# Activation table sets asked for ahead of their use, and the last scaling in four uneven parts

## The reference

```python
def first_block(x, c, ctx, c_ctx, ...):      # one layer
    h = rmsnorm(x) * (1 + scale) + shift      # modulation from c; the same for ctx with c_ctx
    p = h @ w_in                              # r, k, v, gates, low-rank decay and rate, q, k, v, gates of the second mixer
    # mixer A: RWKV-7 recurrence over 16 heads of 64, forwards and backwards, started from the state of ctx
    decay = exp(-exp(-softplus(-w_log) - 0.5)); kk = k * rsqrt(sum(k*k)); y = scan(...); group norm; silu gate
    # mixer B: chunked gated linear attention, 4 heads, both directions: exp of cumulated log-sigmoids
    mixed = sigmoid(g_a) * (y_a @ w_a) + sigmoid(g_b) * (y_b @ w_b)
    return rmsnorm(x + gate * (mixed @ w_out))
def second_block(x, ...):
    # layer AB: 8 heads of dilated attention, 4 heads of differential attention with an RMS norm per head
    # layer C:  16 heads of blockwise attention (all blocks fit, so causal attention)
    # every layer: softmax (exp), silu gate, output projection, residual
    return rmsnorm(h, final_norm)
```

## Time and profile before

| | |
|---|---|
| three executions | 2341.84, 2342.4, 2343.54 us |
| median | 2342.4 us |
| profiled execution, first to last instruction | 2339.4 us |
| DVE, ACT and POOL busy | 1223.0, 1178.4 and 1344.6 us (52, 50 and 57% of the span) |
| ACT_TABLE_LOADs | 63 of 1283 ns |

### The profile page before, as it was taken

The page is one execution under the profiler, slowest core; times in us unless marked ns, Lnnn a source line. Parts: engine busy times, 40 slices in busy tenths (PEclk is TensorE's granted clock), DMA queues, the critical chain, the costliest instruction groups (busy, mean ns, idle before and its releaser), DMA issues.

```text
span 2339.4 us, 60054 instructions
## 1 busy us (share of the span) xinstructions
PE 2285.5 (98%) x23364; PEld 1944.0 (83%) x23364; DVE 1223.0 (52%) x2449; ACT 1178.4 (50%) x1999; POOL 1344.6 (57%) x566
## 2 busy tenths in 40 slices
PE   6999999999999999999999999999999999999997
PEld 4787788778877888899999888888888888888886
DVE  2478778877783332465565455454434533333332
ACT  3245545554553443554444555555555555555554
POOL 1113123322232434488888877877778877778785
PEclk8999999999999999999999999999999999999999
DMA  9922112211211223366767555555555555555553
GB/s 388 381 90 69 43 61 71 65 46 55 69 65 59 86 93 102 100 242 239 268 244 244 180 171 173 173 171 174 172 171 172 182 166 177 172 177 172 171 181 134
DMA packets 101247, 360.75 MB, mean 154 GB/s; under 512 B 11184, under 2 KB 14768, under 8 KB 101072
## 3 DMA queue, kind: packets, MB, share of 16 engines
q1 hardware_dynamic: 99872, 356.89, 44.6%
q10 hardware_dynamic: 1200, 1.25, 0.2%
HBM read 356.00 MB, written 2.10 MB: 153 GB/s over the span
## 4 chain that ended last, share of the span: by engine, by line
PE 89%; DVE 2%; ACT 2%; issue 1%; DVEq 0%; ACTq 0%
PE ps L223 32%; PE ps L224 16%; PE ps L678 5%; PE ps L196 4%; PE ps L198 4%; PE ps L197 4%; PE ps L680 4%; PE ps L679 4%; PE ps L808 1%; PE ps L793 1%; PE ps L829 1%; PE ps L965 1%; PE ps L843 1%; PE ps L939 1%; PE ps L955 1%; PE ps L984 1%
## 5 line engine op out<-in xcount | busy, mean ns | idle before, releaser
L187 POOL TENSOR_TENSOR wlo<-raw,whi 128x1024 fp32r<-128x1024 f32 x555 | 1339.2, 2426 | 941.3 <-ACT whi L178 898.1
L223 PE MATMUL ps<-acts,whi 128*128 128x512 f32 x3072 | 1088.5, 398 | 1.3 <-DVE acts L2777 1.3
L224 PE MATMUL ps<-acts,wlo 128*128 128x256 f32 x3072 | 856.9, 279 | 0.0
L178 ACT ACTIVATE whi<-raw 128x1024 fp32r<-128x1024 f32 x562 | 591.7, 1054 | 270.2 <-PE ps L224 138.8
L223 PEld LDWEIGHTS ps<-acts,whi 128*128 128x128 f32 x3072 | 576.3, 188 | 132.4 <-DVE acts L2777 1.6
L224 PEld LDWEIGHTS ps<-acts,wlo 128*128 128x128 f32 x3072 | 579.1, 188 | 0.9
L678 PE MATMUL ps<-acts,whi 128*128 128x512 f32 (+1 forms) x560 | 217.1, 388 | 1.8 <-DVE W L1543 0.9
L680 PE MATMUL ps<-acts,wlo 128*128 128x512 f32 (+1 forms) x560 | 189.9, 339 | 0.0
L679 PE MATMUL ps<-acts,whi 128*128 128x512 f32 (+1 forms) x560 | 189.8, 339 | 0.0
L196 PE MATMUL ps<-acts,whi 128*128 128x256 f32 (+1 forms) x576 | 181.7, 315 | 0.0
L198 PE MATMUL ps<-acts,wlo 128*128 128x256 f32 (+1 forms) x576 | 180.0, 313 | 0.0
(11 more groups left out here) (391 smaller groups left out, 3085.0 us busy)
## 6 DMA issues: line engine op xcount, KB each, us to landing
raw<-stream SPq DMA_DIRECT2D x564, 512.0 KB, 3.3
W<-stream SPq DMA_DIRECT2D x64, 512.0 KB, 9.2
graw<-stream SPq DMA_DIRECT2D x32, 512.0 KB, 4.4
W<-xT SPq DMA_DIRECT2D x4, 1024.0 KB, 8.7
XR<-xT SPq DMA_DIRECT2D x16, 128.0 KB, 5.6
outT<-XR SPq DMA_DIRECT2D x4, 512.0 KB, 3.3
cns<-consts SPq DMA_DIRECT2D x1, 928.0 KB, 11.0
cns<-consts SPq DMA_DIRECT2D x1, 896.0 KB, 7.4
```

Source lines behind the costliest of these rows:

```text
L178: nc.scalar.activation(high, raw[slot], ACT.Copy).then_inc(hi_done, 1)
L187: nc.gpsimd.tensor_tensor(wlo[slot], raw[slot], whi[slot].bitcast(F32), ALU.subtract).then_inc(lo_done, 1)
L223: nc.tensor.matmul(both_parts, whi[slot][:, k, :], hl[:, :, k0 + k, :], start=first and k == 0, stop=False)
L224: ins = nc.tensor.matmul(ps[:, bank, 0:T], wlo[slot][:, k, :], hl[:, 0, k0 + k, :], start=False, stop=last and k == UK - 1)
```

## The change

Two names of table sets are defined: `LN_EXP` (logarithm and exp) and `EXP_TANH`. ACT is told to load a set with `preload_act_table_set`, an instruction of its own in ACT's queue with no wait. The end's scaling is cut into parts of 2, 2, 4 and 4 tiles on DVE, and SyncE stores each of them by itself; POOL's four tiles are stored after the third part.

```diff
+        LN_EXP, EXP_TANH = "natural_log_exp_and_others", "exp_and_others"
@@ act_inverse (8 times)
             turned(4, 1)
+            nc.scalar.preload_act_table_set(EXP_TANH)
             token_key(1)
@@ act_scan (7 times: not for the last pair)
             solved(2)
+            nc.scalar.preload_act_table_set(LN_EXP)
             act_pad_r(act, j)
@@ act_gla
                 if i == 0:
                     act_square(act, PAIRS - 1)
+                if i == 0:
+                    nc.scalar.preload_act_table_set(LN_EXP)
                 G["gk_mm"].wait(act, 2 * i + 2)
...
                     nc.scalar.activation(zg[:, T * n:T * n + T], z_held(i, n), ACT.Tanh, scale=0.5).then_inc(G["tz"].sem, 1)
+                nc.scalar.preload_act_table_set(LN_EXP)
                 if i + 1 < GH:
                     hi(15)
@@ out_phase, act_
+                            if i == KT // 2 - 1 and n == 0 and base == S_OUT3:
+                                nc.scalar.preload_act_table_set(LN_EXP)
                             tile(i, n)
                         if i == KT // 2 - 1 and k == 5:
-                            nc.scalar.activation(small[:, 106:107], kst_[:, 3:4], ACT.Ln if base == S_OUT3 else ACT.Sqrt)
+                            if base != S_OUT3:
+                                nc.scalar.activation(small[:, 106:107], kst_[:, 3:4], ACT.Sqrt)
@@ dve_final
+        END_PARTS = ((4, 2), (6, 2), (8, 4), (12, 4))
-            for k in range(4, KT, 4):
-                nc.vector.tensor_tensor(XR[:, k:k + 4, :], XR[:, k:k + 4, :],
-                                        ps[:, 7, 0:T].unsqueeze(1).broadcast_to([P, 4, T]), ALU.mult).then_inc(N["x"].sem, 1)
+            for k, n in END_PARTS:
+                nc.vector.tensor_tensor(XR[:, k:k + n, :], XR[:, k:k + n, :],
+                                        ps[:, 7, 0:T].unsqueeze(1).broadcast_to([P, n, T]), ALU.mult).then_inc(N["x"].sem, 1)
@@ sp_store
-            for k in (4, 8, 0, 12):
-                if k:
-                    S["out3"]["x"].wait(sp, k // 4)
-                else:
-                    S["out3"]["tab"].wait(sp, 1)
-                sp.dma_start(outT[:, k:k + 4, :], XR[:, k:k + 4, :]).then_inc(stored, 16)
-            sp.wait_ge(stored, 64)
+            for m, (k, n) in enumerate(END_PARTS):
+                S["out3"]["x"].wait(sp, m + 1)
+                sp.dma_start(outT[:, k:k + n, :], XR[:, k:k + n, :]).then_inc(stored, 16)
+                if m == 2:
+                    S["out3"]["tab"].wait(sp, 1)
+                    sp.dma_start(outT[:, 0:4, :], XR[:, 0:4, :]).then_inc(stored, 16)
+            sp.wait_ge(stored, 16 * len(END_PARTS) + 16)
```

## The result

The changed kernel took 2348.63 us (median of 9 executions, 2346.91 to 2350.64), the kernel before 2342.4 (9 executions, 2340.97 to 2345.13). The ratio is 1.0024, interval 1.0016 to 1.0033: about 5.6 us slower (3.7 to 7.7), or 6.2 by the two medians. The kernel is slower beyond doubt; whether by more than the prediction's 0.2% is open, since the interval reaches to both sides of that. The forecast was 2346.1, +3.7. The sign held, and so did the waits that it named; the size was short by 1.9 us by the ratio and 2.5 by the medians. The profiled execution had a span of 2346.6 us.

A forecast was written before the change was run, and what follows sets the result against it. TensorE, busy 2285.5 of 2339.4 us, was taken as the bound. A to F summed to +3.6 to +3.7, a span of 2343.1 us, plus 3.0 around it: 2346.1, range over the cases 2339.5 to 2351.0.

The forecast's parts named there:

- A: Pair 0's prologue: the explicit load ahead of the squares shifts DVE, partly offset by idle time that goes; +0.24 us.
- B: Scan, seven times: load ahead of L1056 delays PE's L730 by 0.59 us, 0.27 comes back; +2.2 us.
- C: Inversion level 4, eight times: a load delays L1123 and so PE's L786 by 0.17 us each; +1.3 us.
- D: Last gla head: two loads make L1870, and PE's L1768 behind it, late; first three heads have room; +1.5 us.
- Merge: Merge loop: a load at the Tanh of L2067 fits in ACT's 1.67 us of idle; cost 0.
- E: Diff: load between Tanh and Square delays PE's L2636, 0.26 us in three heads, 1.42 in the last; +0.9 us.
- F: The end: log/exp set in place early gives -2.45 us, the smaller store parts about 0.1; -2.55 us.
- only the end counts: Rival, chance 0.13: PE's own queue of matmuls absorbs the waits of B to E; 2339.9 us.
- The cover is gone: Rival, chance 0.18: removed stalls are not regained, +7.1 us, 2349.5; 10.3 more if merge's Tanh lies bare.
- The change doesn't do what it says: Rival, chance 0.05: the build still places its own loads, explicit ones come on top, the end keeps 2.45; about 2351 us.
- a load asked for holds ACT longer: Rival, chance 0.01: an explicit load holds ACT longer than an implicit one, say twice 1.28 us; about 2368 us.
- what was to come earlier behind ACT: Rival, chance 0.08: DVE work awaiting ACT in gla heads and pairs comes earlier, up to 10.4 us back; 2336 us.

The follow-up runs named there:

- e6: Kernel before with only diff's load asked for ahead, between Tanh and Square: 2346.02 us, ratio 1.0021.
- e3: Kernel before with only the loads asked for in gla and diff: 2347.91 us, ratio 1.0021.
- e1: Kernel before with only the end changed, log/exp set loaded ahead of the last tiles and five stored parts: 2340.59 us, ratio 0.9987.
- e10: Kernel before with only the pairs' loads, at the moved places: 2341.22 us, ratio 0.9992.
- e12: Kernel before with only diff's Square done in 8 pieces of 64 columns, signalling after the last, no load added: 2342.6 us, ratio 0.9996.
- e9: Kernel before with only diff's load asked for ahead, behind the Square and the split that follows: 2338.43 us, ratio 0.9984.
- e8: e4 with the end in parts of 2, 2, 2, 2 and 4 tiles: one execution, 8.75 us from PE's last matmul to the span's end.
- e11: The program of e8, timed against the kernel before: 2334.8 us, ratio 0.9968.
- e4: The whole change with its loads at other places, against the kernel before: 2338.98 us, ratio 0.9978.
- e5: Kernel before with only gla's loads asked for ahead: 2343.39 us, ratio 1.0005.

## Why the prediction was right in sign and short in size

- **A** (+0.24): the loads came where they were put, and the first step of the offset in pair 0 was +0.16 (1.18 to 1.34). By 196 us the offset was back at 0.96, so whether A cost anything is not shown.
- **B** (+2.2): PE's start of L730 moved by 0.67 and not 0.59 (PE began 0.14 after L1058's end, 432.65 to 432.79, where I had taken 0.05), and 0.27 came back. 7 x 0.40 = 2.8. **C** (+1.3): 0.17 each, 1.4. Right. The pairs alone measured +4.0, interval 1.9 to 6.1, for A, B and C together 3.7.
- **D** (+1.5): 1.6 in two of three traces, 3.2 in the third, where the clock fell; +1.2 (-0.9 to 3.3) timed. The first three heads had the room. **Merge** (0): the offset did not grow there (+4.90 at 994 us, +4.60 over the stage); the loads stood at L208, in idle time too.
- **E** (+0.9) is the term that was mis-sized: +4.9 measured alone (e6), 2.8 to 7.0; gla and diff together measured the same +4.9 (e3), which less gla's 1.2 leaves 3.7. Its waits came as worked out, 0.26 or 0.27 three times, +1.42 and then -1.48 at L223. What was missing is what PE does after a wait. Behind PE's restart the next 25 us ran in the longer rhythm in 8 of 9 heads, 0.58 us with L2638's own 0.10 in each of e6's three; and after the 2.9 us wait the clock fell in two of three traces, 1.5 us. That makes 0.7 + 1.7 + 1.0 (two thirds of 1.5) = 3.4, an estimate inside the interval; of the 4.9, 1.5 have no row.
- **F** (-2.55): -2.57 in the trace, -3.0 (0.9 to 5.1) timed. The parts brought 0.10, as worked out.
- **Together** the experiments give +4.0 (pairs), +4.9 (gla and diff) and -3.0 (end), 5.9 us, against 5.6 for the whole change. Each is uncertain by some 2 us; within that no large term is missing from the list.
- **The time around the span** was taken as 3.0 us, from one span and three other executions. It is 1.9: e1's profiled execution took 2338.19 us with a span of 2336.3, the changed kernel's 2348.41 with 2346.6, and the others are alike. The profiled execution of the kernel before therefore took some 2341.2 us, 1.2 below its median. Adding 3.0 did no harm to the forecast, which is the median before plus 3.7; as time around the span it was wrong.
- **A pause behind a load**: no row shows one. Between the end of the load at 432.25 and L1058 at 432.26 there is 0.01 us. The Trainium skill (page "ScalarE: Activation LUTs", section "What ACT_TABLE_LOAD costs") adds a drain of about 1380 ns to each switch; this case's traces do not agree, and by that figure the 17 loads would have cost an estimated 23 us more, where 5.6 were measured for the whole change.
- **The rivals**: "only the end counts" falls with the waits of L730. "The cover is gone" was wrong in its mechanism (the 0.27 came back, `merge` stayed covered), although its 2349.5 lay nearer to the 2348.63 than the forecast's 2346.1 did; that was luck. "The change doesn't do what it says" falls with 49 loads and the end's 2.57 us, and "a load asked for holds ACT longer" with the 0.01 us above. Of what was to come earlier behind ACT nothing is left in the changed kernel's time; with the loads moved, PE came 0.9 us earlier in pair 0 of e10's trace.
- **One misreading**: the 3.0 us of idle at L1092 in the earlier trace rows are a total, and 2.9 of them stand ahead of the load in pair 0. The other seven follow at once on ACT's own work. No term hung on it.

What stays open: why PE has two rhythms and what picks one at a restart; e12 was to tell a late Square from a load there and did not. That a load ahead of the Square goes with the longer rhythm is shown; that lateness is the cause is argued. The 2.4 us by which e9 gained more than its wait are open as well, the lower end of its interval being 0.3 above it. `out2` and `out3` ran in the shorter rhythm in e9, e8 and e11 but not in e4, which may be part of it: both together are 3.1 us. Four traces don't show that the moved load brings it.

## What to carry to other kernels

An explicit table load is an instruction of 1.28 us in ACT's queue: put it where ACT is idle, behind the eviction that the busy engine waits for and not ahead of it. With the same 49 loads and the same end, the kernel was 0.24% slower or 0.22% faster by the places of the loads alone. And a new wait of TensorE can cost more than its length: look for a fall of the granted clock and for the spacing of matmuls behind it, and check with a run in which that stage alone is changed. Do not subtract two single traces to price a few microseconds: here they differed by up to 3 us in stages whose program was the same.

## What the runs showed of the hardware

- TensorE at a granted clock of 1.00 showed two spacings for the same pair of matmuls, 346.7 and 353.3 ns on average, each kept over some 90 us of `out2` and of `out3` (after, e3). The same program had either there, 1.6 us each (before and e1; e4 and e8).
- The granted clock fell to 0.50 (1.2 GHz) after waits of 1.94 us (e12), 2.41 (e5) and 2.93 (e3, e6), and stayed at 1.00 after 1.51 (before, e9), 2.40 (changed, e3) and 2.93 (changed). The fall came from 0.4 us before PE resumed (e3) to 1.1 us after (e6), lasted some 3 us and cost 1.4 to 1.6 us; in e12 nearly all of that came back.
- A further ACTIVATE of 128x64 in a row of eight cost some 0.1 us (e12: 1.01 us for eight), not the 0.24 that I had taken from pairs of them.
- An ACT_TABLE_LOAD took 1283 ns wherever it stood, and an ACTIVATE ready to run began 0.01 to 0.03 us behind it (432.25 to 432.26 in the changed kernel).
